# Hybrid encoder trunk on one core: output projection over four open column pairs, with the recurrence spread between the weight splits

## What is computed

```python
proj = rmsnorm(x, mix_norm_e) @ w_in_e
x_br, gate_br, q, k, v = split(proj)
x_br = causal_depthwise_conv(x_br, conv_w, conv_b)
r = sigmoid(x_br @ w_a + b_a); i = sigmoid(x_br @ w_x + b_x)     # block diagonal
log_a = -8 * r * softplus(-lam)
a = exp(log_a); u = sqrt(-expm1(2 * log_a)) * (i * x_br)
h = scan over frames of  h = a * h + u
y_lru = h * gelu(gate_br)                    # 1024 channels
y_att = sliding_window_attention(q, k, v)    # 1024 channels
x = x + concat(y_lru, y_att) @ w_out_e       # the out projection
x = x + square(relu(rmsnorm(x) @ w_up)) @ w_down
```

## Time and profile before

| what | value |
|---|---|
| median of 3 runs | 2130.55 us (2125.67 to 2131.43) |
| the profiled execution | 2124.87 us, span 2123.1 us |
| PE busy | 2038.8 us, 96% |
| DVE busy | 1344.0 us, 63% |
| ACT busy | 941.0 us, 44% |
| POOL busy | 722.4 us, 34% |
| mean granted TensorE clock | 0.983 of full speed |

### The profile page before, as it was taken

One profiled execution on the slowest core, in us unless ns is written; L12 is line 12 of the kernel. 1 busy time (PEld: TensorE's weight loads), 2 busy tenths in 40 slices (PEclk: granted clock), 3 DMA queues, 4 the chain that ended last, 5 costly groups with the idle time before them and its releaser, 6 DMA issues.

```text
span 2123.1 us, 38021 instructions
## 1 busy us (share of the span) xinstructions
PE 2038.8 (96%) x13955; PEld 1761.2 (83%) x13955; DVE 1344.0 (63%) x1515; ACT 941.0 (44%) x1244; POOL 722.4 (34%) x1084
## 2 busy tenths in 40 slices
PE   8989699999999999999986999999999999999998
PEld 7778588888887888888875888888888888888887
DVE  6876667755665576566656766676556656655653
ACT  6345544444443444444451254444444444444443
POOL 2152126888988888860233411100000000000000
PEclk9989899999999999999997999999999999999999
DMA  7534475666665665676784665556565555655664
GB/s 216 164 102 130 116 201 182 196 196 208 207 197 191 193 210 188 218 229 216 259 257 155 199 198 179 181 182 191 187 182 184 191 185 177 196 184 177 194 188 130
DMA packets 374602, 399.99 MB, mean 188 GB/s; under 512 B 23152, under 2 KB 367488, under 8 KB 370400
## 3 DMA queue, kind: packets, MB, share of 16 engines
q1 hardware_dynamic: 366912, 371.77, 56.5%
q0 software_dynamic: 5216, 24.52, 3.8%
q10 hardware_dynamic: 2368, 2.24, 0.3%
HBM read 371.87 MB, written 25.17 MB: 187 GB/s over the span
## 4 chain that ended last, share of the span: by engine, by line
PE 75%; POOL 14%; DVE 4%; issue 3%; ACT 2%; DMA 1%; ACTq 0%; DVEq 0%; POOLq 0%
PE ps L600 46%; PE ps L602 23%; POOL t L1895 1%; PE px L882 1%; POOL t L1894 1%; DVE Wl L1286 1%; POOL stg L1896 1%; POOL t L1893 1%; POOL stg L1897 1%; POOL t L1892 1%; PE px L864 1%; ACT Wh L964 1%; PE ps L901 1%; DMA raw<-in_w_out_e_dram 1%; POOL t L1869 1%
## 5 line engine op out<-in xcount | busy, mean ns | idle before, releaser
L600 PE MATMUL ps<-A,Wh 128*128 128x512 f32 x5152 | 1815.7, 401 | 21.9 <-DVE A L1610 17.7
L602 PE MATMUL ps<-A,Wl 128*128 128x256 f32 x5152 | 1397.9, 282 | 0.0
L1286 DVE TENSOR_TENSOR Wl<-raw,Wh 128x1024 fp32r<-128x1024 f32 x660 | 834.8, 1277 | 607.5 <-ACT Wh L964 600.9
L600 PEld LDWEIGHTS ps<-A,Wh 128*128 128x128 f32 x5152 | 953.5, 189 | 235.5 <-issue 21.6
L964 ACT ACTIVATE Wh<-raw 128x1024 fp32r<-128x1024 f32 x660 | 689.2, 1057 | 788.2 <-PE ps L602 511.7
L602 PEld LDWEIGHTS ps<-A,Wl 128*128 128x128 f32 x5152 | 977.1, 190 | 29.2
L1786 POOL TENSOR_TENSOR sq<-xT 128x512 f32 (+1 forms) x24 | 31.2, 1299 | 335.3 <-DVE xT L1711 152.8
L1122 ACT ACTIVATE A<-cross 128x512 f32 (+1 forms) x64 | 40.4, 632 | 204.3 <-DVE cross L1626 204.3
L1357 DVE TENSOR_TENSOR cross<-ps,cross 128x512 f32<-128x512 f32 x163 | 111.3, 683 | 9.4 <-ACT cross L968 9.2
L968 ACT ACTIVATE cross<-ps 128x512 f32<-128x512 f32 x165 | 95.9, 581 | 12.7 <-PE ps L600 9.6
L1629 DVE TENSOR_TENSOR A<-cross,A 128x512 f32 (+1 forms) x64 | 47.1, 737 | 57.4 <-ACT A L1122 57.4
(11 more groups left out here) (310 smaller groups left out, 1261.8 us busy)
## 6 DMA issues: line engine op xcount, KB each, us to landing
raw<-in_w_up_dram SPq DMA_DIRECT2D x256, 512.0 KB, 3.9
raw<-in_w_down_dram SPq DMA_DIRECT2D x256, 512.0 KB, 4.6
raw<-in_w_glu_dram SPq DMA_DIRECT2D x64, 512.0 KB, 4.6
raw<-in_w_in_e_dram SPq DMA_DIRECT2D x52, 512.0 KB, 3.8
raw<-in_w_out_e_dram SPq DMA_DIRECT2D x32, 512.0 KB, 4.5
s_params<-stg POOLq DMA_DIRECT2D x16, 1024.0 KB, 5.4
slot<-s_params SPq DMA_DIRECT2D x16, 1024.0 KB, 6.2
xin<-in_x_dram SPq DMA_DIRECT2D x4, 512.0 KB, 7.9
```

The costliest lines, as they stand in the source:

```text
L600: wide = lambda: mm(ps[:, b + t, :], Wh[:, s, c, cols], A[:, k, :], start=(n == 0), stop=(n == KC - 1))
L602: half = lambda: mm(ps[:, b + t, 0:L], Wl[:, s, c, cols], A[:, k, 0:L], start=False, stop=False)
L1286: tt(Wl[:, s], raw[:, s], Wh[:, s].bitcast(F32), ALU.subtract).then_inc(lo_split, 1)
```

## The change

In the out projection PE now keeps four pairs open at once: two in `ps`, and two in the four banks of `px`, which attention and the gate products have left by then. `out_unit(u)` gives pair and contraction block of unit u: units 0 to 7 are the two attention blocks of pairs 0 to 3, units 8 to 11 the first recurrence block of the four pairs, units 12 to 15 the second. Pairs 4 to 7 follow as before. SP loads in that order.

```diff
+        def out_unit(u):
+            return (u // 2, 2 + u % 2) if u < 8 else (u % 4, (u - 8) // 4)
+        def out_banks(p):
+            b = 2 * ((P_OUT + p) % 2)
+            return ps[:, b:b + 2, :] if p < 2 else px[:, 2 * (p - 2):2 * (p - 2) + 2, :]
...
-            pair(P_OUT, P_OUT % 2, A2, turn=2, ready=a2_ready, base=0, per_unit=4)
-            double_pairs(pe, 7, lambda j, d: pair(j + (P_OUT + 1), (P_OUT + 1 + d) % 2, A2, turn=2), last=1)
+            for u in range(4 * NU):
+                p, s = out_unit(u)
+                if u == 0:
+                    pe.wait_ge(pair_read, P_OUT - 1)
+                if u == 2:
+                    pe.wait_ge(pair_read, P_OUT)
+                if u == 4:
+                    pe.wait_ge(gates_sg, LC)
+                if u == 6:
+                    pe.wait_ge(p_copied, LC)
+                pe.wait_ge(lo_split, P_OUT * NU + u + 1)
+                pe.wait_ge(a2_ready, {2: 4, 3: 8, 0: 12, 1: 16}[s])
...
+            for j in range(4):
+                pair(P_OUT + 4 + j, (P_OUT + j) % 2, A2, freed=P_OUT + 1 + j if j < 2 else None)
```

On ACT the tanh of each gate moves up to the next unit (units 23 to 30), and splits stand between the parts of the recurrence:

```diff
                 if 0 <= n - GATE0 < LC:
+                    if n == GATE0:
+                        act.wait_ge(lru_sp, 1)
+                    else:
+                        gate_tanh(n - GATE0 - 1)
                     gates(n - GATE0)
                 if n == GATE0 + LC:
-                    act.wait_ge(gates_sg, LC)
-                    act.wait_ge(lru_sp, 1)
-                    for c in range(LC):
-                        fn(lt[:, c], lr[:, c], ACT.Tanh, scale=ls[:, 4, c:c + 1])
+                    gate_tanh(LC - 1)
...
+            out_split(4)
+            decay_root(0)
+            out_split(5)
+            decay_root(1)
+            out_split(6)
             act.wait_ge(g_ready, 4)
             for c in range(0, LC, 4):
                 fn(gT[:, c:c + 4], gT[:, c:c + 4], ACT.Gelu_apprx_tanh).then_inc(lru_h, 1)
+            out_split(7)
+            lru_high(0)
+            out_split(8)
+            out_split(9)
+            out_split(10)
+            lru_high(1)
+            for u in range(11, 16):
+                out_split(u)
+            for p in range(4):
+                out_split(16 + p)
+                act.wait_ge(unit_done, P_OUT * NU + 13 + p)
+                cross_terms((P_OUT + p) % 2, out_banks(p))
+                if p >= 1:
+                    operand_from_x(p - 1, G_FF0)
+            operand_from_x(3, G_FF0)
```

On DVE the two products of `li` (L1582) and the two squares (L1588) are gone, the recurrence is cut into steps per half, and splits of units 4 to 10 stand between them; the four open pairs are evicted one after another, each behind one split:

```diff
+            last_gate()
+            decay_gain(0)
+            out_split(4)
+            decay_gain(1)
+            out_split(5)
+            lru_input(0)
+            out_split(6)
+            lru_scan(0)
+            out_split(7)
+            lru_gated(0)
+            lru_low(0)
+            out_split(8)
+            lru_input(1)
+            out_split(9)
+            lru_scan(1)
+            out_split(10)
+            lru_gated(1)
+            lru_low(1)
+            for u in range(11, 16):
+                out_split(u)
+            for p in range(4):
+                out_split(16 + p)
+                c = (P_OUT + p) % 2
+                evict(P_OUT + p, c, banks=out_banks(p))
+                residual(p, c)
+                if p >= 1:
+                    operand_from_x(p * 2 - 2, G_FF0)
+            operand_from_x(6, G_FF0)
```

POOL takes them over, ahead of its wait for `a2_ready`:

```diff
+            for c in range(LC):
+                pool.wait_ge(gates_sg, c + 1)
+                tt(li[:, c], li[:, c], xc[:, c], ALU.mult).then_inc(lru_u, 1)
+            for c in range(0, LC, 4):
+                pool.wait_ge(lru_a, c + 4)
+                tt(la[:, c:c + 4], lr[:, c:c + 4], lr[:, c:c + 4], ALU.mult).then_inc(lru_sq, 1)
```

More of the change, by code:

```diff
@@ L478, in _ @@
                 load_pair(j + P_XB, w_in, 0, j * TW)
-            for j in range(8):
-                load_pair(P_OUT + j, w_out, 0, j * TW, turn=2)
+            for u in range(4 * NU):
+                p, s = out_unit(u)
+                sp.wait_ge(lo_split, P_OUT * NU + u - NU + 1)
+                src = w_out[s * UK * P:(s + 1) * UK * P, p * TW:(p + 1) * TW]
+                sp.dma_start(raw[:, u % NU], src.rearrange("(c p) n -> p c n", p=P)).then_inc(landed[u % NU], 16)
+            for j in range(4, 8):
+                load_pair(P_OUT + j, w_out, 0, j * TW)
             load_mlp(P_MLP0, 0, QTR - 1)
@@ L583, in first_unit, with pair @@
                 last.then_inc(unit_done, 1)
-            def pair(g, d, A, ready=None, base=0, per_unit=0, turn=0, beside=None):
+            def pair(g, d, A, ready=None, base=0, per_unit=0, turn=0, beside=None, freed=None):
                 b = 2 * d
-                if not (isinstance(g, int) and g < 2):
+                if freed is not None:
+                    pe.wait_ge(pair_read, freed)
+                elif not (isinstance(g, int) and g < 2):
                     pe.wait_ge(pair_read, g - 1)
@@ L1056, in attended, with gate_tanh @@
                 hi.inc(fn(A2[:, LC + i, 0:L], px[:, 3, 0:L], ACT.Copy))
+            def gate_tanh(c):
+                act.wait_ge(gates_sg, c + 1)
+                fn(lt[:, c], lr[:, c], ACT.Tanh, scale=ls[:, 4, c:c + 1])
             def gates(c):
@@ L1593, in _ @@
                 dest = xb[:, 2 * j:2 * j + 2, 3:3 + L] if j < 4 else gT[:, 2 * j - 8:2 * j - 6, :]
[L1594 to L1600, removed]
-                link(tt(li[:, h], li[:, h], lt[:, h], ALU.mult))
-                for k in range(c, c + 4):
+                if g < P_OUT - 1:
+                    pair(g, g % 2, beside=lambda s: beside(j * NU + s))
+                    tt(dest, cross[:, g % 2], rs2, ALU.mult).then_inc(xb_ready if j < 4 else g_ready, 1)
@@ new lines, in _, with out_split, last_gate, decay_gain @@
+            for s in range(NU):
+                split(P_OUT, s)
+                beside(7 * NU + s)
+            def out_split(u):
+                split(P_OUT + u // NU, u % NU)
+            def last_gate():
+                g = P_OUT - 1
+                evict(g, g % 2)
+                tt(gT[:, LC - 2:LC, :], cross[:, g % 2], rs2, ALU.mult).then_inc(g_ready, 1)
+            def decay_gain(h):
+                c = slice(4 * h, 4 * h + 4)
+                dve.wait_ge(lru_sq, h + 1)
+                stt(lt[:, c], la[:, c], 1.0, lt[:, c], ALU.add, ALU.mult).then_inc(lru_m2, 1)
@@ L1606, in _, with lru_gated, lru_low @@
-                for k in range(c, c + 4):
+            def lru_gated(h):
+                dve.wait_ge(lru_h, h + 1)
+                for k in range(4 * h, 4 * h + 4):
                     tt(gT[:, k], gT[:, k], la[:, k], ALU.mult).then_inc(lru_y, 1)
-            for c in range(LC):
-                hi.wait(dve)
-                tt(A2[:, c, L:2 * L], gT[:, c], A2[:, c, 0:L].bitcast(F32), ALU.subtract).then_inc(a2_ready, 1)
+            def lru_low(h):
+                for c in range(4 * h, 4 * h + 4):
+                    hi.wait(dve)
+                    tt(A2[:, c, L:2 * L], gT[:, c], A2[:, c, 0:L].bitcast(F32), ALU.subtract).then_inc(a2_ready, 1)
```

78 lines of the change are left out of this document (49 added, 29 removed).

## The result

| | before | after |
|---|---|---|
| median | 2130.98 us (2122.8 to 2135.72, 10 runs) | 2116.16 us (2112.02 to 2124.87, 10 runs) |
| ratio, 95% interval | | 0.9942 [0.9926, 0.9959] |
| profiled execution, span | 2124.87 us, 2123.1 us | 2112.86 us, 2111.1 us |
| POOL busy | 722.4 us | 735.0 us |
| last evict of the out projection starts | 336.28 us | 322.84 us |

The change makes the kernel faster by 0.58% (0.41% to 0.74%). 2116 was predicted. The runs of one kernel spread by some 13 us, and the longer ones have the lower mean granted clock (2112.02 us at 0.989, 2124.87 us at 0.981), so medians of a few runs don't tell 2 us apart.

The account below looks back on a forecast made before the run. PE was taken to bound the kernel, time being won only at its gaps, low clock or an earlier POOL chain. Losses 1.4 + 1.8 + 4.5 + 1.7 + 1.7 = 11.1 against 25.0 us: gain 14, median 2116, range 2107 to 2124.

Parts of the forecast that it names:

- Where the time was: Out projection stage, 225.71 to 335.6 us: 30 units of PE at 2.83 us are 84.9 us, so 25.0 us are lost.
- Restart: Seam of the two projections: unit 2 needs the last gate pair's evict, ended at 227.1 us; PE loses 1.4 us.
- The train: DVE's interleaved recurrence steps and splits, 228.4 to 254.4 us; PE wants unit 11 at 252.6 us and loses 1.8 us.
- Closing four pairs: Units 12 to 15 end one unit apart; DVE's rounds of 4.6 us delay unit 20 and PE loses 4.5 us.
- the prediction's own sign: Expected in the profile after: PE has no gap over 5 us between 220 and 330 us.
- The weights of unit 16: Loaded from 255.6 us beside POOL's first table load, taken as 8 us, so landed at 263.6 us.
- The clock: Low clock behind the gap from closing four pairs, at unit 20: 1.7 us lost.
- The second batch: Second table loads, 267 to 284 us, meet weights of units 21 to 23; hidden, with 1 to 3 us to spare.
- Behind the stage: POOL's parameter chain and PE's later wait hang on the out projection's end, so a gain there reaches the program's end.
- The low clock by going through the banks: Rival "Slower": changing banks unit by unit keeps the clock low, 2.83 us more for each of 16 units, 2162 us; chance 0.03.
- Nothing collides: Rival: POOL doesn't hold up DVE, loads take 4.5 us; losses 4.7, gain 20, time 2110 us; chance 0.20.
- The collisions add up: Rival: squares at 3.8 us, second batch bites, two low-clock stretches; gain 6 us, time 2124 to 2125; chance 0.12.

Follow-up runs that it names:

- the run without squares: The changed kernel with the squares of the decays and the `li` products back on DVE instead of POOL; ratio 0.9942 to the kernel before.
- the second profile: The changed kernel itself, unaltered, run once more beside the kernel before; 2118.93 us, ratio 0.9956.
- the GpSimd part alone: The kernel before with only the `li` products and squares of the decays moved to POOL, one pair open; ratio 1.0004.
- both edits: The changed kernel with POOL's table loads and squares after the fourth residual, splits of units 20 and 21 ahead of operand parts; ratio 0.9896, again 0.9938.

## Why the prediction was right

**Where the time was.** "From 225.71 to 335.6 us are 109.9 us", 25.0 of them lost, 11.1 to be lost after. 11.4 were. Cutting the stage to PE's units at 2.83 us, and asking of each loss whether it stays, was what made the number: units 2 to 10 took 25.7 us by the trace (227.18 to 252.90), 25.5 by the sum.

**Restart**, 1.4: 1.39. Exact, since each of its four steps has a row in the trace before. The tanh cost nothing: PE ran dry at 225.79 us, against 225.71 before.

**The train**, 1.8: 0.91. The term was mis-sized in several small pieces. Two squares on POOL took 3.74 us, not 4.2, and held DVE for 0.8 us, not 1.3, so the scaling was done at 228.69 us and not 229.1; the rest of the train was some 0.2 us shorter than its sum, and PE asked for unit 11 at 252.90 and not 252.6. The direction holds: the scaling began at 227.16 us, inside a square that ended at 228.14 us, and took 1.53 us and not the 0.69 of the run without squares. By the Trainium skill (SBUF — State Buffer, "SBUF: two separate sides") the later of two such instructions waits for the port until the earlier one is done. The trace agrees in size: 0.84 us lost, near the 1.0 us that was left of the square.

**Closing four pairs**, 4.5: 5.26, and here the mechanism was only half right. The step that failed is "one operand part (1.91)", and with it the rounds of "4.6 us against PE's 2.83". The 1.91 us were not the cost of the instructions. This is the kernel before around that row, DVE and then POOL:

```profile
327.96 1.91 DVE L1375 SCALAR_TENSOR_TENSOR A<-xT,pcol,A  x2 [1.44 <-ACT A L992]
...
327.90 1.29 POOL L1787 TENSOR_TENSOR ss<-ss,sq 128x512 f32<-128x512 f32 x1
```

POOL's sum of the same residual had begun 0.06 us earlier. Two operand parts in that trace that ran beside nothing of POOL took 0.88 us:

```profile
256.14 0.88 DVE L1375 SCALAR_TENSOR_TENSOR A<-xT,pcol,A  x2 [1.50 <-ACT A L992]
```

So it is in all twelve traces of this case: 0.87 or 0.88 us for two that begin while POOL computes nothing (270.00 and 273.26 us after), 1.68 to 2.74 where it is at work (1.80 at 325.95 us, beside the sum of 325.77). In the closing rounds POOL was still issuing table loads, so a round took 3.3 us, and with such rounds alone unit 20 is in time (0.31 us of waiting with the squares later). The bill came behind them, in one piece: four residuals' squares, and DVE held for 5.5 us. The sum thus had a hold-up of 1.03 us in each round without knowing it, 4.1 us in four; what came was 5.5 us after the rounds. That the gap came out near the sum is luck: it is owed to this likeness, not to the argument. It was even over the 5 us that the prediction's own sign set as the limit for any gap (5.26 and 5.08 us).

**The weights of unit 16**, 263.6 us: ACT split them at 262.48 us. Those of unit 17 took 10.37 us, under the 12 us set as the limit. The sum had no term for them; they held DVE's rounds back by 1.41 us, on the way to unit 20.

**The clock**, 1.7: 2.1, and 3.1 in the second profile. **The second batch**, hidden with 1 to 3 us to spare: hidden, but only because PE stood at unit 20. ACT got unit 22's weights at 285.96 us; once the gap was taken away, PE waited 2.2 and 2.9 us for them. It was no spare time.

**Behind the stage**: "a gain there reaches the end" held but for 1.4 us. PE's wait of 4.72 us for POOL stayed, but an earlier one of 1.36 us came up. From the last evict PE got to that place in 179.6 us before and 179.7 us after, while POOL's last `bp` (L1871, L2009) was done 178.2 us behind it before and 181.0 us after: POOL's chain had been in time by 1.4 us and was then late by as much. The wait isn't the price of the shorter stage, since it also stands in the run with the GpSimd part alone, whose last evict (334.96 us) comes only 1.3 us sooner than before; of all other runs only the one with late table loads alone is without it. Why the chain takes longer stays open. So the sum's 14 us became 12.0 in the span. That the median came out at 2116 all the same is luck: it stands 3.3 us above the profiled execution after, instead of the 5.7 that were assumed.

**The rivals.** The low clock by going through the banks is ruled out: it is 1.00 from 226 to 282 us, units 8 to 15 included, which change to other banks at each unit. "Nothing collides" fell, since unit 20 waited 5.26 us. "The collisions add up" didn't come: the squares took 1.9 us each and not 3.8, one low-clock stretch came and not two, and the second batch of table loads cost nothing as long as PE stood at unit 20.

## What to carry over

An idle PE at a seam is filled by units that don't need the late operand, if their weights and banks are there too: opening more accumulators without interleaving the weight splits made this kernel slower, and both together took the stage's losses from 25.0 to 11.4 us. A duration taken from a trace holds for the neighbours it ran beside: look what the other engines do in that row before it goes into a sum. In this kernel work of GpSimd was not free when it was off the path: ask at each place where VectorE is short what GpSimd does then, above all what it will catch up on after a stall. A small stall in front can hide a second one behind it, so a fix is worth the difference to the next in line, not the length of the gap.

## What was not expected of the hardware

- VectorE and GpSimd hold each other up, and not by a few per cent: beside GpSimd's products and sums four splits take 7.40 and 7.63 us instead of 4.6, two operand parts up to 2.74 instead of 0.88, and GpSimd's own product 1.79 to 2.13 instead of 1.04 us. Both lose.
- The hold-up was in the trace before for whoever put two timelines side by side: 0.88 us at 256.14, 1.91 us at 327.96, the same instructions.
- Between its first two table loads GpSimd did nothing for 12.46 us, and the profile names no wait for it (10.75 before); with the loads later it was 8.81 to 10.09 us.
- Whether the clock falls behind a short gap isn't decided by its length: 2.67 us with two pairs open were followed by a low clock, 2.68 us with both edits not.
